# Second mixer of a fused transformer block: the attention heads' small products stand in 10 places between the projections' matmuls in place of 16

## What is computed

```python
def stick_breaking(q, k, v):
    ...
        z = jnp.einsum('bthd,bshd->bhts', qb, k).astype(jnp.float32) * d_h ** -0.5
        ...
        lo = jnp.where(mask, jax.nn.log_sigmoid(-z), 0.0)
        rc = lax.cumsum(lo, axis=3, reverse=True)
        log_a = jax.nn.log_sigmoid(z) + (rc - lo)
        a = jnp.where(mask, jnp.exp(log_a), 0.0)
        return jnp.einsum('bhts,bshd->bthd', a.astype(v.dtype), v)

def mixer_c(n, w_in, gq, gk, w_out):
    q, k, v = _split(n @ w_in, (C_WIDTH, C_WIDTH, C_WIDTH))
    q = rmsnorm(q.reshape(bsz, s_len, N_HEADS_C, HEAD_DIM), gq)
    k = rmsnorm(k.reshape(bsz, s_len, N_HEADS_C, HEAD_DIM), gk)
    ...
    return stick_breaking(q, k, v).reshape(bsz, s_len, C_WIDTH) @ w_out
```

## Time and profile before

| | |
|---|---|
| Median of 3 runs (lowest, highest) | 948.35 us (948.12, 949.17) |
| The profiled execution, its span | 947.72 us, 945.8 us |
| TensorE matmuls busy | 936.3 us, 99% |
| VectorE busy | 712.4 us, 75% |
| ScalarE busy | 595.6 us, 63% |
| TensorE on the chain that ended last | 94% |
| Second mixer's projections on TensorE | from about 317 to 397 us of the span |

### The profile page before, as it was taken

How to read it: one execution, slowest core, us unless ns; L and a number is a source line. 1 busy time by engine, 2 the same in 40 slices (tenths; PEclk the granted TensorE clock), 3 DMA queues, 4 the chain that set the end, 5 groups by cost and what they waited for, 6 DMA issues and landing times.

```text
span 945.8 us, 14580 instructions
## 1 busy us (share of the span) xinstructions
PE 936.3 (99%) x5944; PEld 832.4 (88%) x5944; DVE 712.4 (75%) x1034; ACT 595.6 (63%) x869; POOL 36.2 (4%) x15
## 2 busy tenths in 40 slices
PE   9999999999999999999999999999999999999997
PEld 7888888888888888888888888899999999999886
DVE  5997846777988867747787988776568789898643
ACT  7676548888655658748888645734555596555532
POOL 0021250000000000020000000000000000000000
PEclk9999999999999999999999999999999999999999
DMA  8554244555555552445554556454544437555541
GB/s 305 222 190 161 91 137 176 191 201 188 185 215 204 184 192 92 175 143 186 197 190 178 196 205 220 148 186 171 178 162 162 167 134 245 178 179 182 194 159 44
DMA packets 25345, 168.22 MB, mean 178 GB/s; under 512 B 2816, under 2 KB 3904, under 8 KB 5568
## 3 DMA queue, kind: packets, MB, share of 16 engines
q1 hardware_dynamic: 24848, 166.84, 49.4%
q10 hardware_dynamic: 432, 0.46, 0.1%
HBM read 166.24 MB, written 1.05 MB: 177 GB/s over the span
## 4 chain that ended last, share of the span: by engine, by line
PE 94%; DVE 3%; ACT 2%; DMA 1%; issue 1%; SPq 0%; DVEq 0%; ACTq 0%
PE bank L724 23%; PE bank L725 23%; PE bank L726 23%; PE bank L833 12%; PE bank L837 6%; DVE wlo L1996 1%; PE bank L752 1%; DMA raw<-w_stream 1%; PE bank L887 0%; PE bank L1106 0%; ACT whi L1339 0%; PE bank L891 0%; PE bank L895 0%; PE bank L1240 0%; PE bank L1132 0%
## 5 line engine op out<-in xcount | busy, mean ns | idle before, releaser
L1996 DVE TENSOR_TENSOR wlo<-raw,whi 128x2048 fp32r<-128x2048 f32 (+2 forms) x136 | 303.7, 2234 | 132.2 <-ACT whi L1339 131.9
L1339 ACT ACTIVATE whi<-raw 128x2048 fp32r<-128x2048 f32 (+1 forms) x139 | 264.6, 1905 | 99.7 <-PE bank L726 97.6
L833 PE MATMUL bank<-nhl,whi 128*128 128x512 f32 x512 | 124.2, 392 | 0.2 <-DVE nhl L2009 0.2
L833 PEld LDWEIGHTS bank<-nhl,whi 128*128 128x128 f32 x512 | 93.9, 188 | 19.4 <-issue 0.7
L724 PE MATMUL bank<-mhi,whi 128*128 128x258 f32 x384 | 108.4, 282 | 0.4 <-DVE mlo L2705 0.4
L725 PE MATMUL bank<-mlo,whi 128*128 128x258 f32 x384 | 108.4, 282 | 0.0
L726 PE MATMUL bank<-mhi,wlo 128*128 128x258 f32 x384 | 108.2, 282 | 0.0
L724 PE MATMUL bank<-nhl,whi 128*128 128x258 f32 (+3 forms) x320 | 92.3, 288 | 0.4 <-DVE nhl L2009 0.4
L725 PE MATMUL bank<-nhl,whi 128*128 128x258 f32 (+3 forms) x320 | 91.4, 286 | 0.0
L726 PE MATMUL bank<-nhl,wlo 128*128 128x258 f32 (+3 forms) x320 | 90.5, 283 | 0.0
L724 PEld LDWEIGHTS bank<-mhi,whi 128*128 128x128 f32 x384 | 72.5, 189 | 0.8 <-issue 0.8
(11 more groups left out here) (388 smaller groups left out, 1907.0 us busy)
## 6 DMA issues: line engine op xcount, KB each, us to landing
raw<-w_stream SPq DMA_DIRECT2D x154, 1024.0 KB, 4.8
h<-x_rows SPq DMA_DIRECT2D x4, 256.0 KB, 4.7
raw<-w_stream SPq DMA_DIRECT2D x2, 512.0 KB, 5.9
cst<-consts SPq DMA_DIRECT2D x1, 832.0 KB, 6.3
e<-g_post SPq DMA_DIRECT2D x1, 512.0 KB, 7.0
out_rows<-e SPq DMA_DIRECT2D x2, 256.0 KB, 2.0
raw<-w_stream SPq DMA_DIRECT2D x1, 352.0 KB, 9.4
vec<-vectors SPq DMA_DIRECT2D x1, 258.5 KB, 8.9
```

Of the source, the lines that this page charges most:

```text
L833: return pe.matmul(us[c].t[:, :], w[:, k, c * P:c * P + P].hi, nboth[:, k, :], start=k == 0, stop=k == 7)
L1339: act.activation(whi[j][:, 0:n], raw[j][:, 0:n], ACT.Copy).then_inc(s_hi.up(i))
L1996: dve.tensor_tensor(wlo[j][:, 0:m], raw[j][:, 0:m], whi[j][:, 0:m].bitcast(F32), ALU.subtract).then_inc(s_lod.up(i))
```

## The change

Only the table `STICKS` is changed. The turn of head group 0 goes from behind quarter (7, 2) to (8, 1), ahead of turn 1. Query-key product 0 goes from (8, 2) to (8, 3). Key sums 0 go from (9, 1) to (9, 2). Turn 2 goes from (9, 1) to (10, 1), ahead of key sums 2 and turn 3. Query-key product 6 goes from (10, 3) to (11, 0), ahead of key sums 4. Value product 2 goes from behind (11, 3) to ahead of output tile 0, where product 3 stands, and products 6 and 7 go from output tile 2 to 1. The programs of the other engines stay as they are; the banks are handed out anew from the table.

```diff
--- before.py
+++ after.py
@@ -255,23 +255,17 @@
 
 
 STICKS = {
-    (7, 2): [("cT", 0)],
-    (8, 1): [("cT", 1)],
-    (8, 2): [("sz", 0)],
-    (8, 3): [("sz", 1)],
-    (9, 1): [("sr", 0), ("cT", 2)],
-    (9, 2): [("sz", 2), ("sr", 1)],
+    (8, 1): [("cT", 0), ("cT", 1)],
+    (8, 3): [("sz", 0), ("sz", 1)],
+    (9, 2): [("sr", 0), ("sz", 2), ("sr", 1)],
     (9, 3): [("sz", 3)],
-    (10, 1): [("sr", 2), ("cT", 3)],
+    (10, 1): [("cT", 2), ("sr", 2), ("cT", 3)],
     (10, 2): [("sr", 3), ("sz", 4), ("sz", 5)],
-    (10, 3): [("sz", 6)],
-    (11, 0): [("sr", 4), ("sz", 7)],
+    (11, 0): [("sz", 6), ("sr", 4), ("sz", 7)],
     (11, 1): [("sr", 5), ("sv", 0)],
     (11, 2): [("sr", 6), ("sr", 7), ("sv", 1)],
-    (11, 3): [("sv", 2)],
-    ("out", 0): [("sv", 3)],
-    ("out", 1): [("sv", 4), ("sv", 5)],
-    ("out", 2): [("sv", 6), ("sv", 7)],
+    ("out", 0): [("sv", 2), ("sv", 3)],
+    ("out", 1): [("sv", 4), ("sv", 5), ("sv", 6), ("sv", 7)],
 }
```

## The result

The changed kernel takes 971.9 us (median of 5 runs, 971.42 to 972.83) against 948.33 of the kernel before: a ratio of 1.0251, 95% interval 1.024 to 1.0263. Its profiled execution took 971.48 us, span 969.6.

A forecast was written before the change was run, and what follows sets the result against it. TensorE was taken as the bound, busy 936.3 of 945.8 us. Waits of 6.8 + 0.2 + 11.6 + 0.7 + 1.25 = 20.6 us plus 2.45 for the clock gave 23.05, so 971.4 us; range 967.5 to 975.5.

The forecast's parts named there:

- the total: Whole kernel: waits summing to 20.6 us plus 2.45 us for TensorE's clock, giving 971.4 us.
- the second wait: TensorE at key sums 2, behind turn 2 at (10, 1): some 10 us wait; this move loses 11.6 us.
- such a term: TensorE's clock falls in both large waits, 3.15 us at half speed behind each: 2.45 us loss in all.

The follow-up runs named there:

- the run of turn 0 alone: Kernel before with only turn 0 moved from (7, 2) to (8, 1), ahead of turn 1: 956.41 us, ratio 1.0087.
- that of turn 2 alone: Kernel before with only turn 2 moved from (9, 1) to (10, 1), ahead of key sums 2 and turn 3: 960.95 us, ratio 1.0137.
- the one with ScalarE's first order mended: Changed kernel with squares 1, copy of tile 57 and factors 1 put ahead of turn 0's evacuation on ScalarE: 963.0 us, ratio 1.0156.
- the first try with filler matmuls: Changed kernel plus 14 no-result matmuls ahead of turn 1 and 21 ahead of key sums 2, the latter into key sums 2's bank: 976.25 us, ratio 1.0295.

## What to carry to other kernels

When a step is moved on one engine and another engine's order is written out by hand, look at what stands *behind* that step's consumer in the other engine's queue: if a later step of the first engine needs it, two steps put side by side wait for the whole chain between them, here 7 and 10 us. Grouping small matmuls between large ones of the same engine saved nothing that shows; mending the other engines' order gave the loss back, and no more. Walking the three queues forward with start-to-start times from the trace of before gave the total within 0.5 us.

## What was not expected of the hardware

The clock's timing moved from run to run. Counted from TensorE's last work it fell 4.6 and 4.2 us later in the changed kernel, but 2.4 in the run of turn 0 alone, 2.0 in that of turn 2 alone, 4.1 in the one with ScalarE's first order mended, and 3.15 at the end of the kernel before. After TensorE resumed it came back 4.5 and 4.5, then 5.7, 5.7 and 4.4 us later. In the first try with filler matmuls the second wait has 4.0 and, from the filler's start, 3.2. So one fall read in one trace gives such a term only roughly. And a stretch at half clock costs less than its slow matmuls when the next limit is another engine: 1.7 us of slow work behind the second wait cost 0.8. Filler matmuls kept the clock at full level through both waits, but only where their bank was free: filler that waited for a bank made the kernel 4.3 us slower.
